# A mixture-of-experts kernel: second weight loaded as two neighbouring rows per partition, activations transposed with a stride of 8

## The reference, cut to what matters

```
def expert_block(args):
    xblk, e = args
    hdn = xblk @ w1[e] + b1[e]                       # 1024 -> 2048
    gate = jnp.minimum(hdn[..., :D_FF], SWIGLU_LIMIT)
    lin = jnp.clip(hdn[..., D_FF:], -SWIGLU_LIMIT, SWIGLU_LIMIT)
    act = gate * jax.nn.sigmoid(SWIGLU_ALPHA * gate) * (lin + 1.0)
    return act @ w2[e] + b2[e]                       # 1024 -> 1024
```

## Time and profile before

| what | value |
|---|---|
| median of three executions | 2283.36 us |
| the profiled execution | 2282.82 us |
| its span, first to last instruction | 2281.1 us |
| PE busy | 2056.2 us (90%) |
| DVE busy | 1622.5 us (71%) |
| ACT busy | 1221.7 us (54%) |
| HBM read | 512.87 MB |

### The profile page before, as it was taken

How to read it: one execution, slowest core, us unless ns; L and a number is a source line. 1 busy time by engine, 2 the same in 40 slices (tenths; PEclk the granted TensorE clock), 3 DMA queues, 4 the chain that set the end, 5 groups by cost and what they waited for, 6 DMA issues and landing times. The chain is left out here.

```text
span 2281.1 us, 26251 instructions
## 1 busy us (share of the span) xinstructions
PE 2056.2 (90%) x9338; PEld 1628.6 (71%) x9338; DVE 1622.5 (71%) x1524; ACT 1221.7 (54%) x1045; POOL 249.4 (11%) x172
## 2 busy tenths in 40 slices
PE   6899896968777899996999999999999999999992
PEld 4766565756656688873788888888888888888881
DVE  4643527676666522535899999999999999899982
ACT  5433324151524332321677777777777777777763
POOL 0000003324251200000010000101000000000100
PEclk9999997979797999995999999999999999999996
DMA  4221224423232294353899999999999999999982
GB/s 131 58 74 56 74 56 138 139 74 130 83 120 79 68 326 157 111 192 120 311 360 369 368 365 377 365 371 359 370 374 361 375 362 368 362 371 365 367 304 81
DMA packets 212050, 541.09 MB, mean 237 GB/s; under 512 B 16438, under 2 KB 131544, under 8 KB 175064
## 3 DMA queue, kind: packets, MB, share of 16 engines
q1 hardware_dynamic: 204600, 518.54, 62.6%
q0 software_dynamic: 7392, 21.77, 4.0%
HBM read 512.87 MB, written 31.59 MB: 239 GB/s over the span
## 5 line engine op out<-in xcount | busy, mean ns | idle before, releaser
L1860 DVE TENSOR_TENSOR w_low<-ring_b,w_high 128x2048 fp32r<-128x2048 f32 x192 | 436.0, 2288 | 44.3 <-ACT w_high L1854 44.0
L1860 DVE TENSOR_TENSOR w_low<-ring_a,w_high 128x2048 fp32r<-128x2048 f32 x192 | 435.5, 2287 | 43.0 <-ACT w_high L1854 42.8
L1854 ACT ACTIVATE w_high<-ring_b 128x2048 fp32r<-128x2048 f32 x192 | 368.2, 1919 | 161.0 <-PE ps L1954 109.8
L1854 ACT ACTIVATE w_high<-ring_a 128x2048 fp32r<-128x2048 f32 x192 | 367.9, 1918 | 151.8 <-PE ps L1954 110.1
L1954 PE MATMUL ps<-w_high,rows_high 128*128 128x512 f32 x1024 | 403.8, 394 | 1.3 <-DVE w_low L1860 1.2
L1954 PE MATMUL ps<-w_high,rows_low 128*128 128x512 f32 x1024 | 400.3, 391 | 0.0
L1954 PE MATMUL ps<-w_low,rows_high 128*128 128x512 f32 x1024 | 399.7, 390 | 0.0
L236 DVE TENSOR_TENSOR unit_low<-unit_raw,unit_high 128x1024 fp32r<-128x1024 f32 x108 | 134.6, 1261 | 126.7 <-ACT unit_high L231 126.5
L2018 PE MATMUL ps<-w_high,act_high 128*128 128x512 f32 x512 | 207.6, 405 | 18.9 <-DVE w_low L1860 18.9
L1954 PEld LDWEIGHTS ps<-w_high,rows_high 128*128 128x128 f32 x1024 | 192.9, 188 | 44.0 <-DVE w_low L1860 4.5
L1954 PEld LDWEIGHTS ps<-w_high,rows_low 128*128 128x128 f32 x1024 | 192.8, 188 | 41.2
(11 more groups left out here) (329 smaller groups left out, 2992.1 us busy)
## 6 DMA issues: line engine op xcount, KB each, us to landing
ring_a<-in_w SPq DMA_DIRECT2D x192, 1024.0 KB, 7.4
ring_b<-in_w SPq DMA_DIRECT2D x192, 1024.0 KB, 7.5
unit_raw<-in_w_in SPq DMA_DIRECT2D x80, 512.0 KB, 4.0
temps<-cum_rows SPq DMA_DIRECT2D x16, 1024.0 KB, 9.1
unit_raw<-in_w_up_ssd SPq DMA_DIRECT2D x16, 512.0 KB, 4.7
ssd_out_T<-y_high SPq DMA_DIRECT2D x4, 1024.0 KB, 4.2
ssd_out_T<-y_low SPq DMA_DIRECT2D x4, 1024.0 KB, 6.0
ssd_high<-ssd_out_T SPq DMA_DIRECT2D x4, 1024.0 KB, 10.5
```

The lines of the kernel that those rows point to most:

```text
L1854: nc.scalar.activation(w_hi[:, split_at(it, j)], slot(at, 1)[:, 0, :], ACT.Copy).then_inc(w_hi_ok, 1)
L1860: nc.vector.tensor_tensor(w_lo[:, split_at(it, j)], slot(at, 1)[:, 0, :], w_hi[:, split_at(it, j)].bitcast(F32), ALU.subtract).then_inc(w_ ...
```

## The change

In load_down the assignment of w2's rows to partitions changes. Before, down tile u held rows 256u + p and 256u + 128 + p on partition p: two separate runs of 4 KB in HBM, and the whole tile was one contiguous megabyte. After, partition p holds rows 8p + 2u and 8p + 2u + 1: one run of 8 KB, and the runs of neighbouring partitions lie 32 KB apart. Piece k of the contraction is now rows k, k + 8, k + 16 and so on, and so acts_pe takes every eighth column of l_w for piece c in place of 128 neighbouring ones. The sums over the pieces add the same 1024 products in another order.

```diff
         def load_down(sp, it, u, to):
 
-            src = w2.rearrange("e k n -> (e k) n")[bass.ds(it % NE * DFF + u * 2 * P, 2 * P), :]
-            sp.dma_start(slot(to, 2), src.rearrange("(k p) n -> p k n", p=P)).then_inc(exp_w[to], 16)
+            src = w2.rearrange("e k n -> (e k) n")[bass.ds(it % NE * DFF, DFF), :].rearrange("(p k) n -> p k n", p=P)
+            sp.dma_start(slot(to, 2), src[:, 2 * u:2 * u + 2, :]).then_inc(exp_w[to], 16)
...
             for c in range(NK):
-                last = nc.tensor.transpose(ps[:, 6 + c // 4, (c % 4) * CAP:(c % 4 + 1) * CAP], l_w[0:CAP, c * P:(c + 1) * P], ident[0:CAP, 0:CAP])
+                last = nc.tensor.transpose(ps[:, 6 + c // 4, (c % 4) * CAP:(c % 4 + 1) * CAP], l_w[0:CAP, bass.ds(c, P, step=NK)], ident[0:CAP, 0:CAP])
             last.then_inc(aT_tp, 1)
```

## The result

The changed kernel took 2294.46 us (median of five, 2290.57 to 2298.41) against 2283.80 us of the kernel before beside it: ratio 1.0046, 95% interval 1.0032 to 1.0061. It is slower by about 10.6 us, and the whole interval lies above 1. Forecast were 2297 us.

What follows compares the result with a forecast made beforehand. The prediction took a closed PE, ACT and DVE cycle to bound the 36.00 us pass. It summed 0 (loads) + 13.7 us (transposes) onto the median 2283.4 us, giving 2297 us, range 2282 to 2318 us.

Steps and rivals of the forecast that it cites:

- The cycle: Expert stage: PE's piece, then ACT and DVE to the last down tile, in series; time added to acts_pe lengthens the 36.00 us pass.
- PE's wait at the last down tile: PE's weight loads waiting for DVE's split, 18.6 us in 28 waits; forecast to stay.
- PE then works through the up tiles at its own pace: After up tile 0: PE runs on unheld, so time added to acts_pe is added to the pass with no cover.
- Part 1, the strided load: Transposes in acts_pe: seven exposed weight loads each 61 ns longer, 0.43 us per pass, 13.7 us over 32 passes.
- a read at half rate: Strided weight loads: throughput part, at most 82 ns, doubles; 61 ns taken as the middle between 40 and 82.
- the 1.25 that I gave as a sign: L1991's eight matmuls: some 1.25 us in place of 0.82 if the forecast was right, with a pass of 36.4 us.
- The DVE row of a strided write: DVE's L1721 against L1727 and L1734: the step costs 90 ns per 128 floats, which would give 20.2 us.
- Part 2, the loads: SP's four w2 loads per pass: 0 us, as even the longest landing, 10.3 us, leaves 7.7 us before use.
- The stride costs PE nothing: Rival at the transposes: slack in the 82 ns hides the longer load, no measurable change, 2283 us; chance 0.34 for none.
- costs much more: Rival at the transposes: DVE step's price or whole pace, 20 to 34 us slower, 2303 to 2317 us; chance 0.19.
- The transfers become the bound: Rival at w2's loads: runs 32 KB apart hit HBM unevenly, ACT waits for landings; 22 to 150 us; chance 0.04.
- The faster case: Rival: a DMA wait, or PE's 0.67 us wait for DVE, shrinks; 2262 us if all 0.67 went; chance 0.05.

Runs made afterwards that it cites:

- the copies moved: DVE's small copies L1893 and L1894, which wait for the scatter, moved behind the split of up tile 6; on the kernel before alone, ratio 0.9994.
- The doubled transposes: Against the kernel before: both groups of eight transposes (L1991 and L1928) with a stride of 8, loads as before; ratio 1.0021.
- the change, copies later: The changed kernel with L1893 and L1894 moved behind the split of up tile 6, against the kernel before: 2288.24 us, ratio 1.0020.
- new loads alone, copies later: Against the kernel before: only w2's new loads, with L1893 and L1894 moved behind the split of up tile 6, transposes as before; ratio 0.9989.
- before, copies later: The kernel before with only L1893 and L1894 moved behind the split of up tile 6, against the kernel before: ratio 0.9994.
- stride 2: Against the kernel before: each down tile a contiguous megabyte, partition p holding rows 256u + 2p and 256u + 2p + 1, transposes taking every second column; ratio 1.0040.
- stride 2, copies later: Contiguous down tiles in 8 KB runs, every second column transposed, L1893 and L1894 behind up tile 6's split, against the kernel before: 2290.07 us, ratio 1.0023.
- stride 4: Against the kernel before: two neighbouring w2 rows per partition out of groups of four, 8 KB runs 16 KB apart, transposes taking every fourth column; ratio 1.0064.

## Why the prediction was right, and where it was not

The time was forecast at 2297 us and came out at 2294.5. That it came so near is luck: two terms were off in opposite directions, 13.7 us forecast for the stride where it costs 5 to 6, and 0 for the loads where they cost 5 to 7.

**The cycle** held where I used it. An operation in PE's piece between the last down tile and the up tiles appears in the pass in full: with the copies moved, where nothing else disturbs it, the passes last 36.18 us on the mean with the stride and 35.99 without, 0.19 us more, for 0.20 us more at acts_pe. PE's wait at the last down tile stayed at 18.7 us, as forecast. The doubled transposes add that the wait is a cover too, for work that lies ahead of it.

But "PE then works through the up tiles at its own pace" was wrong, and the wait for the scatter lies just there. DVE's L1893 stands between its splits of up tiles 5 and 6, and PE takes up tile 6 as soon as DVE has split it. The first two lines are the kernel before (the split of tile 6 ends at about 1628.5, PE's first weight load for it starts at 1628.57), the third is the new loads alone, behind the wait of 1.27 us:

```profile
1626.23 4.49 DVE L1860 TENSOR_TENSOR w_low<-ring_b,w_high 128x2048 fp32r<-128x2048 f32 x2
```

```profile
1628.57 0.19 PEld L1954 LDWEIGHTS ps<-w_high,rows_high 128*128 128x128 f32 x1
```

```profile
1310.67 0.19 PEld L1954 LDWEIGHTS ps<-w_high,rows_high 128*128 128x128 f32 x1 [1.38 <-DVE w_low L1860]
```

So the cycle has a third point where one engine hands over to another with nothing to spare, and a wait of DVE ahead of it lengthens the pass: 1.27 us of wait, and 37.23 us.

**Part 1, the strided load**, was right in its place and its mechanism (the load grows beyond what is covered, and sets the pace) and too large. I had taken 61 ns more per load, and it was 64 (204 against 140). This too is luck: 61 was the middle of a span for a read at half rate, and no run shows a half rate; the strides from 2 to 8 cost from 58 to 91 ns, and a stride of 2 more than one of 8 (217 against 204 ns among their like).

The error lies in what I made of it. I let each nanosecond count from 82 ns on, seven times: 0.43 us per pass. Measured are 0.16 to 0.20 us, as the matmuls now start 0.107 us apart on the mean, 0.025 more than before. So some 35 to 40 ns of each load's growth didn't reach the pace; that this much had been slack under the matmul is how I read it. Hence the eight matmuls took 1.02 us and not the 1.25 that I gave as a sign, and the pass 36.2 us and not 36.4. From the first to the last product L1984 there are 31 passes, and 31 by 0.18 us are 5.6 us; the transposes alone measured 5, and 13.7 were forecast. The DVE row of a strided write, 90 ns per 128 numbers, would have been further off.

**Part 2, the loads**, failed. "The sum holds 0 for it" rested on the tiles' own landing, and that was right: no engine ever waited for a tile, and 32 KB of distance with runs of 4 KB cost nothing. What I missed is who shares the DMA engines. The scatter lies on another queue, it is in flight just while the four down tiles are loaded (from 1610.94 on, the scatter from 1615.16), and DVE waits for it ahead of its split of up tile 6.

The row was there, L1893 with 1.4 us in four waits, and I read it as the most that could be gained. A wait that is short and appears in some passes only is a margin of nearly nothing, and a later landing by 0.3 us goes straight through it. The traces give the margin: from the scatter's start until DVE is ready for L1893 there are 9.37 us in the kernel before (median of 28). 4 of its 28 scatters take over 9.4 us to land, and 11 of 28 with the new loads alone. Two runs show it: the same loads with the copies moved cost nothing (0.9989), and the same addresses in 4 KB runs neither (1.0005).

The two costs also touch each other. With strided transposes L1893 comes later, while the scatter still starts 7.80 us behind the product L1984. So the margin is 9.55 us with the strided transposes alone and 9.62 us in the changed kernel, and L1893 waits 4.3 us there and 8.0 us with the loads alone.

The ledger, with the pass's growth from PE (0.18 us for a stride of 8, 0.25 for 2 and 4, by 31) and the waits of L1893 less the 1.4 us of before. The last column is what the traces show directly, the time from the first to the last product L1984 less the 1118.2 us of the kernel before:

| kernel | stride on PE | wait for scatter | sum | measured (ratio - 1) x 2284 | in the trace |
|---|---|---|---|---|---|
| the change | 5.6 | 2.9 | 8.5 | 10.5 | 10.1 |
| strided transposes alone | 5.6 | -0.5 | 5.1 | 5.3 | 5.0 |
| new loads alone | 0 | 6.6 | 6.6 | 6.6 | 7.7 |
| same addresses, 4 KB | 0 | -1.1 | -1.1 | 1.1 | -1.2 |
| the change, copies later | 5.6 | -1.4 | 4.2 | 4.6 | 3.9 |
| new loads alone, copies later | 0 | -1.4 | -1.4 | -2.5 | -1.7 |
| before, copies later | 0 | -1.4 | -1.4 | -1.4 | -1.9 |
| stride 2 | 7.8 | 0.4 | 8.2 | 9.1 | 9.1 |
| stride 2, copies later | 7.8 | -1.4 | 6.4 | 5.3 | 6.0 |
| stride 4 | 7.8 | 6.0 | 13.8 | 14.6 | 15.5 |

Sum and measurement agree within 2.2 us in all ten, and the intervals of the measurement are 2 to 3 us to either side, so rows that differ by less than that are not told apart. The waits and the last column come from one execution each, while the times are medians over several.

**The rivals.** "The stride costs PE nothing" was wrong, "costs much more" too. "The transfers become the bound" was wrong as put: neither bandwidth nor the distance. A wait for a transfer was part of the answer, but for one that I hadn't listed. The faster case, a shorter wait for DMA, was the same wait with the wrong sign.

None of the complete versions here is measurably faster than the kernel before. In every layout tried, runs of 8 KB came with a stride in the transposes, and its 5 us are more than they give.

## What to carry to other kernels

Before a load is called free because nothing waits for it, look at every other transfer that is in flight at that time and at how close its waiter is: a wait that appears in a few passes only says that the margin is all but gone. The length of a run on one queue was felt on another. And a weight load of 96 x 128 float32 numbers with a stride of 2 to 8 took some 60 to 90 ns longer than one of neighbouring numbers, which is free as far as the matmul or an existing wait covers it, and is paid in full elsewhere.

## What the runs showed of the hardware that I had not expected

- Weight loads of 96 x 128 float32 numbers for a transpose: 140 ns with neighbouring numbers, 198 to 231 ns with strides from 2 to 8. A stride of 2 (217 ns in a row of its kind) costs more than one of 8 (204 ns). The note on lines of 16 bytes in the Trainium skill (SBUF — State Buffer, section on the DMA port swizzle) would have a stride of 2 float32 free; the runs disagree. Why a stride costs what it does stays open.
- Runs of 8 KB in place of 4 KB on one queue moved the median landing of a scatter on another from 9.0 to 9.3 us (9.5 us with a contiguous tile, 9.8 us with 16 KB between the runs), with the same bytes and nearly the same rate (366 and 365 GB/s from 1200 to 2220 us). At the same addresses in 4 KB it was 9.0 again.
- A distance of 32 KB between the partitions' runs in HBM cost nothing that can be measured (ratio 1.0005 with runs of 4 KB; 0.9989 with runs of 8 KB and the waiting copies moved).
